# RMS norms from row sums on 128x9 numbers, applied behind the projections, in a hybrid decoder step

## The reference, cut to what matters

```
def rms_norm(x, g):
    y = x * rsqrt(mean(x * x, axis=-1) + 1e-6)
    return y * g

mixed = (g_a * (o_nsa @ w_branch_nsa) + g_b * (o_gm @ w_branch_gm)) @ w_out
x = x + rms_norm(mixed, ln_mix_post)
h2 = rms_norm(x, ln_ffn_pre)
f = (silu(h2 @ w_ffn_gate) * (h2 @ w_ffn_up)) @ w_ffn_down
x = x + rms_norm(f, ln_ffn_post)
e = ple @ w_ple
x = x + rms_norm(sigmoid(x @ w_ple_gate) * e, ln_ple_post)
```

## Time and profile before

| | us |
|---|---|
| median of 3 runs (2498.2 to 2499.25) | 2499.18 |
| the profiled execution | 2501.11 |
| its span, first to last instruction | 2499.3 |

### The profile page before, as it was taken

How to read it: one execution, slowest core, us unless ns; L and a number is a source line. 1 busy time by engine, 2 the same in 40 slices (tenths; PEclk the granted TensorE clock), 3 DMA queues, 4 the chain that set the end, 5 groups by cost and what they waited for, 6 DMA issues and landing times. The chain is left out here.

```text
span 2499.3 us, 33749 instructions
## 1 busy us (share of the span) xinstructions
PE 2152.2 (86%) x13578; PEld 2008.8 (80%) x13578; DVE 767.1 (31%) x1412; ACT 491.0 (20%) x881; POOL 628.7 (25%) x487
## 2 busy tenths in 40 slices
PE   7999799688768888799997909999999999992992
PEld 6999799587656667688887808999999999992882
DVE  3006233121256676311114184100111111127116
ACT  4111022100126656300102121111000100011121
POOL 2224100000024444212113123323323323223122
PEclk8999799756669999899998959999999999996996
DMA  5241431224020000111111221111111111120111
GB/s 179 61 148 39 127 136 59 79 102 168 6 110 2 1 1 1 34 50 38 38 42 51 84 85 51 40 45 51 50 38 55 42 37 56 44 100 28 40 34 68
DMA packets 164092, 151.17 MB, mean 60 GB/s; under 512 B 24010, under 2 KB 156555, under 8 KB 161156
## 3 DMA queue, kind: packets, MB, share of 16 engines
q1 hardware_dynamic: 160308, 116.41, 15.2%
q0 software_dynamic: 2304, 33.56, 3.5%
q10 hardware_dynamic: 1392, 0.01, 0.0%
HBM read 133.04 MB, written 21.10 MB: 62 GB/s over the span
## 5 line engine op out<-in xcount | busy, mean ns | idle before, releaser
L500 PE MATMUL ffn_acc<-HH,WS 128*128 128x344 f32 x2112 | 393.9, 321 | 21.2 <-POOL WS L510 18.8
L508 POOL CAST WS<-W 128x1024 fp32r<-128x1024 f32 (+2 forms) x126 | 129.8, 1030 | 1092.8 <-PE ffn_acc L500 508.8
L500 PEld LDWEIGHTS ffn_acc<-HH,WS 128*128 128x128 f32 x2112 | 344.7, 189 | 23.4 <-POOL WS L510 19.8
L510 POOL TENSOR_TENSOR WS<-W,WS 128x1024 fp32r<-128x1024 f32 (+2 forms) x126 | 293.5, 2330 | 10.1
L500 PE MATMUL ffn_acc<-HL,WS 128*128 128x344 f32 x1056 | 224.8, 321 | 0.0
L500 PE MATMUL ffn_acc<-AH,WS 128*128 128x344 f32 x1056 | 195.4, 320 | 0.0
L500 PE MATMUL proj_acc<-HH,WS 128*128 128x344 f32 x912 | 174.4, 324 | 7.6 <-DVE HL L474 7.6
L500 PEld LDWEIGHTS ffn_acc<-HL,WS 128*128 128x128 f32 x1056 | 179.4, 190 | 0.0
L1721 POOL TENSOR_SCALAR Hr<-Hr,tiny,gtok 128x63 f32<-128x63 f32 (+4 forms) x192 | 125.1, 661 | 185.4 <-DVE tiny L1801 141.5
L500 PEld LDWEIGHTS ffn_acc<-AH,WS 128*128 128x128 f32 x1056 | 171.7, 188 | 0.0
L2133 DVE TENSOR_TENSOR E<-E,ffn_acc 128x1032 f32<-128x1032 f32 x22 | 27.1, 1230 | 469.9 <-PE ffn_acc L500 469.9
(11 more groups left out here) (354 smaller groups left out, 3328.8 us busy)
## 6 DMA issues: line engine op xcount, KB each, us to landing
W<-in_w_in SPq DMA_DIRECT2D x31, 512.0 KB, 4.2
W<-in_w_ffn_gate SPq DMA_DIRECT2D x22, 512.0 KB, 3.8
W<-in_w_ffn_up SPq DMA_DIRECT2D x22, 512.0 KB, 3.8
X<-kept_x SPq DMA_DIRECT2D x2, 4128.0 KB, 13.2
W<-in_w_ffn_down SPq DMA_DIRECT2D x16, 384.0 KB, 3.4
W<-in_w_ffn_down SPq DMA_DIRECT2D x16, 320.0 KB, 3.2
kept_x<-Z SPq DMA_DIRECT2D x1, 4128.0 KB, 13.9
Z<-kept_x SPq DMA_DIRECT2D x1, 4128.0 KB, 13.0
```

What stands on the lines that cost most here:

```text
L500: last = k.nc.tensor.matmul(acc[:, s, n, 0:NW], k.WS[:, ws, part, c, :], src[:, c, n * NW:(n + 1) * NW], start=(c == 0 and part == 0 and s ...
L508: k.nc.gpsimd.tensor_copy(k.WS[:, ws, 0, 0:nk, :], w).then_inc(hi_done, 1)
L510: k.nc.gpsimd.tensor_tensor(k.WS[:, ws, 1, 0:nk, :], w, k.WS[:, ws, 0, 0:nk, :].bitcast(F32), ALU.subtract).then_inc(split_done, 1)
```

## The change

The four `norm_stage` calls go. `row_sums` takes the mean of the squares with tokens on the partitions: for each of nine token blocks the squares are the stationary operand and one column of 1/1024 moves, so that the result is 128x9. `RowRoot` adds eps, takes the reciprocal and the root on these numbers, and `row_spread` turns them back into a 128x1032 pattern in PSUM.

- Out-projection's norm: sums and spread at the head of `ffn`, then chunk by chunk scale, add and split (`first_tile` and the lists of ACT and DVE beside it).
- The FFN's pre-norm: only the gain stands ahead of the projections; the squares of each chunk are summed on PE between the chunks of the first gate tile, and the root (`k.R1`) is applied to the gate's result twice, ahead of the silu and behind it.
- The FFN's post-norm: at the head of `ple`, chunk by chunk.
- The last norm: the gain is applied to `k.F` in the loop of `ple`; x and F are both transposed in `store_y`, and there the root is a scale per token.
- The first tile of w_out is fetched and split at the end of `merge`; `out_projection` is written out instead of looped, ACT squares from PSUM and then copies. x is spilled by ACT's queue in `ffn`.

```diff
         merge(k)
         out_projection(k)
-        norm_stage(k, "mix_post", k.MX, residual=1, onto=k.MT, known=True)
-        norm_stage(k, "ffn_pre", k.X, spill=True)
         ffn(k)
-        norm_stage(k, "ffn_post", k.F, residual=3, onto=k.X, known=True)
         ple(k)
-        norm_stage(k, "ple_post", k.F, residual=4, onto=k.X, known=True)
         store_y(k)
...
+def row_sums(k, ps, sq, first=True, last=True):
+    for t in range(9):
+        m = P if t < TT else B
+        x = k.nc.tensor.matmul(ps[0:m, t:t + 1], sq[:, t * P:t * P + m], k.ones[:, 0:1], start=first, stop=last)
+    return x
+def row_spread(k, flat, rs):
+    for t in range(9):
+        m = P if t < TT else B
+        x = k.nc.tensor.matmul(flat[:, t * P:t * P + m], rs[0:m, t:t + 1].to_broadcast([m, P]), k.ident[0:m, 0:m], start=True, stop=True)
+    return x
+class RowRoot:
+    def __init__(self, k, st, name):
+        self.k = k
+        self.rs = k.tiny[:, 0:9]
+        self.cleared, self.mean, self.inverse, self.rooted = st.sems(" ".join(f"{name}_{x}" for x in ("cleared", "mean", "inverse", "rooted")))
+    def clear(self, dve):
+        self.k.nc.vector.memset(self.rs[:, TT:TT + 1], 1.0).then_inc(self.cleared, 1)
+    def vector(self, dve, ps):
+        nc = self.k.nc
+        dve.wait_ge(self.cleared, 1)
+        dve.wait_ge(self.mean, 1)
+        nc.vector.tensor_scalar(self.rs[:, 0:TT], ps[:, 0:TT], EPS, None, ALU.add).then_inc(self.inverse, 1)
+        nc.vector.tensor_scalar(self.rs[0:B, TT:TT + 1], ps[0:B, TT:TT + 1], EPS, None, ALU.add).then_inc(self.inverse, 1)
+        dve.wait_ge(self.inverse, 2)
+        nc.vector.reciprocal(self.rs, self.rs).then_inc(self.inverse, 1)
+    def scalar(self, act):
+        act.wait_ge(self.inverse, 3)
+        self.k.nc.scalar.activation(self.rs, self.rs, ACT.Sqrt).then_inc(self.rooted, 1)
...
+            sp.wait_ge(split_done, 17)
+            sp.dma_start(k.W[:, 0, 0:8, :], weight(g["w_out"], 0)).then_inc(k.wfull[0], 16)
...
+            pool.wait_ge(k.wfull[0], base[0] + 8 * 32 + 16)
+            pool.wait_ge(scaled, 2 + 15)
+            split_weights(k, pool, 0, 0, DC, hi_done, 16, split_done)
...
-            with sp.Fori(0, 4) as i:
-                for s in range(2):
-                    sp.wait_ge(split_done, 2 * i + s + 1)
-                    sp.dma_start(k.W[:, s, :, :], weight(g["w_out"], (2 * i + s) * P)).then_inc(k.wfull[s], 16)
+            for m in range(1, 8):
+                if m >= 3:
+                    sp.wait_ge(split_done, m - 2)
+                sp.dma_start(k.W[:, m % 2, :, :], weight(g["w_out"], m * P)).then_inc(k.wfull[m % 2], 16)
             sp.wait_ge(m_lo, DC)
             sp.dma_start(k.Z[:, 0:DC * N], k.kept).then_inc(x_back, 16)
             sp.wait_ge(x_back, 16)
...
+            for m in range(1, 8):
+                pool.wait_ge(k.wfull[m % 2], base[m % 2] + 16 * ((m + 1) // 2 if m % 2 else m // 2))
+                if m >= 2:
+                    pool.wait_ge(mm_done, m - 1)
+                split_weights(k, pool, m % 2, m % 2, DC, hi_done, m - 1, split_done)
...
+            for m in range(8):
+                if m:
+                    pe.wait_ge(split_done, m)
+                if m >= 2:
+                    pe.wait_ge(acc_free, m - 1)
+                split_tile(k, acc, m % 2, m % 2, k.HH, k.HL, DC, wait=(pe, m_lo) if m == 0 else None).then_inc(mm_done, 1)
...
+            for m in range(8):
+                act.wait_ge(mm_done, m + 1)
+                squares.square(act, acc[:, m % 2, :, 0:NW], m, m % 2)
+                nc.scalar.activation(tokens(k.MX[:, m, :]), acc[:, m % 2, :, 0:NW], ACT.Copy).then_inc(acc_free, 1)
+            act.wait_ge(acc_free, 8)
...
         done = (gate_done, up_done)
-        free = (silu_done, gated)
+        free = (scaled, gated)
         SL = k.E[:, 0:N]
         GU = k.E[:, N:2 * N]
-        h = NormSplit(k, st, 2, k.E[:, 0:N])
+        h = GainSplit(k, st, 2, k.MT)
+        roots = [RowRoot(k, st, "mix"), RowRoot(k, st, "pre")]
+        zeros = k.E[:, 5400:5409]
+        flat = acc[:, 1].rearrange("p n w -> p (n w)")[:, 0:N]
...
+        def first_tile(pe):
+            row_sums(k, aux[:, 0, 0:9], k.ssq).then_inc(roots[0].mean, 1)
+            pe.wait_ge(roots[0].rooted, 1)
+            row_spread(k, flat, roots[0].rs).then_inc(spread, 1)
+            pe.wait_ge(zeroed, 1)
+            nc.tensor.matmul(aux[:, 1, 0:9], k.ident[:], zeros, start=True, stop=False)
+            pe.wait_ge(split_done, 3)
+            for c in range(DC):
+                pe.wait_ge(h.lo_done, c + 1)
+                last = split_tile(k, acc, 0, 0, k.HH, k.HL, c + 1, first=c, more=c < DC - 1)
+                if c == DC - 1:
+                    last.then_inc(gate_done, 1)
+                pe.wait_ge(squared2, c + 1)
+                row_sums(k, aux[:, 1, 0:9], k.sq[:, c % 2, :], first=False, last=False).then_inc(summed2, 1)
+            nc.tensor.matmul(aux[:, 1, 0:9], k.ident[:], zeros, start=False, stop=True).then_inc(roots[1].mean, 1)
+            pe.wait_ge(roots[1].rooted, 1)
+            pe.wait_ge(mixed, DC)
+            row_spread(k, flat, roots[1].rs).then_inc(spread, 1)
+            pe.wait_ge(r_copied, 1)
...
-            h.scalar(act)
+            roots[0].scalar(act)
+            for c in range(DC):
+                act.wait_ge(x_new, c + 1)
+                h.scalar(act, c)
+                if c >= 2:
+                    act.wait_ge(summed2, c - 1)
+                nc.scalar.activation(k.sq[:, c % 2, :], k.MT[:, c, :], ACT.Square).then_inc(squared2, 1)
+            act.dma_start(k.kept, k.Z[:, 0:DC * N]).then_inc(spilled, 16)
+            roots[1].scalar(act)
+            act.wait_ge(spread, 2)
+            nc.scalar.activation(k.R1[:], flat, ACT.Copy).then_inc(r_copied, 1)
+            act.wait_ge(spilled, 16)
             for nf, m0, t0, s0, d0 in parts:
                 with act.Fori(0, nf) as m:
-                    act.wait_ge(gate_done, m + (m0 + 2))
-                    act.wait_ge(gated, m + (m0 + 1))
-                    nc.scalar.activation(tokens(SL), acc[:, 0, :, 0:NW], ACT.Silu).then_inc(silu_done, 1)
...
-            h.vector(dve)
+            nc.vector.memset(zeros, 0.0).then_inc(zeroed, 1)
+            roots[0].clear(dve)
+            roots[0].vector(dve, aux[:, 0, 0:9])
+            dve.wait_ge(spread, 1)
+            for c in range(DC + 1):
+                if c < DC:
+                    nc.vector.scalar_tensor_tensor(out=k.MX[:, c, :], in0=k.MX[:, c, :], scalar=k.gains[:, 1, c:c + 1], in1=flat,
+                                                   op0=ALU.mult, op1=ALU.mult).then_inc(mixed, 1)
+                    dve.wait_ge(mixed, c + 1)
+                    nc.vector.tensor_tensor(k.MT[:, c, :], k.MT[:, c, :], k.MX[:, c, :], ALU.add).then_inc(x_new, 1)
+                if c:
+                    dve.wait_ge(x_new, c)
+                    h.vector(dve, c - 1)
+            roots[1].clear(dve)
+            roots[1].vector(dve, aux[:, 1, 0:9])
+            dve.wait_ge(r_copied, 1)
+            dve.wait_ge(spilled, 16)
             for nf, m0, t0, s0, d0 in parts:
                 with dve.Fori(0, nf) as m:
+                    dve.wait_ge(gate_done, m + (m0 + 2))
+                    dve.wait_ge(gated, m + (m0 + 1))
+                    nc.vector.tensor_tensor(tokens(SL), acc[:, 0, :, 0:NW], tokens(k.R1[:]), ALU.mult).then_inc(scaled, 1)
                     dve.wait_ge(silu_done, m + (m0 + 2))
+                    nc.vector.tensor_tensor(SL, SL, k.R1[:], ALU.mult).then_inc(rescaled, 1)
+                    dve.wait_ge(rescaled, m + (m0 + 1))
                     dve.wait_ge(up_done, m + (m0 + 2))
...
+        ptok = k.E[:, 0:9 * 256].rearrange("p (t f) -> p t f", f=256)
...
+        root = RowRoot(k, st, "post")
+        flat = acc[:, 1].rearrange("p n w -> p (n w)")[:, 0:N]
...
+            row_sums(k, acc[:, 0, 0, 0:9], k.ssq).then_inc(root.mean, 1)
+            pe.wait_ge(root.rooted, 1)
+            row_spread(k, flat, root.rs).then_inc(spread, 1)
...
+                pe.wait_ge(mixed, DC)
...
+            root.scalar(act)
             for c in range(DC):
+                if c < 6:
+                    f, q = c // 3, c % 3
+                    act.wait_ge(tr_done, c + 1)
+                    a, w = (q * 512, 512) if q < 2 else (T, B)
+                    nc.scalar.activation(pT[:, f, a:a + w], tp[:, c % 2, 0:w], ACT.Copy).then_inc(tr_copied, 1)
+                act.wait_ge(x_new, c + 1)
                 nc.scalar.activation(k.HH[:, c, :], k.X[:, c, :], ACT.Copy).then_inc(x_hi, 1)
...
+                act.wait_ge(squares.squared, m + 1)
+                nc.scalar.activation(one(k.F, m), one(k.F, m), ACT.Copy, scale=k.gains[:, 4, bass.ds(m, 1)]).then_inc(scaled, 1)
...
+            root.clear(dve)
+            root.vector(dve, acc[:, 0, 0, 0:9])
+            dve.wait_ge(spread, 1)
+            for c in range(DC + 1):
+                if c < DC:
```

(61 more changed lines are left out.)

52 lines of the change are left out of this document (9 added, 43 removed).

## The result

The changed kernel takes 2411.0 us (median; 2408.7 to 2415.0) against 2499.2 for the kernel before beside it: a ratio of 0.9647, with a 95% interval from 0.963 to 0.9664. The direction was right and the size was not: 88 us came off instead of 67. The profiled execution took 2408.7 us, its span is 2406.9, against 2501.1 and 2499.3.

A forecast was written before the change was run, and what follows sets the result against it. PE, busy 86% of the span, was taken as the bound, with four holes where savings count one for one. Gains 9.0 + 14.2 + 23.1 + 20.8 = 67.1 us gave 2434.0 profiled, 2432.1 median; range 2418 to 2446.

The forecast's parts named there:

- Where PE waits: Three holes at the late norm stages and a 13.48 us one ahead of the out-projection; savings there shorten the span one for one.
- Ahead of the out-projection, 9.0: Merge and out-projection: early weight fetch and split start PE 7.8 us earlier, squaring from PSUM saves 1.2; together 9.0 us.
- Steps 1 to 4: Head of the FFN: row sums 3.7 us, root 1.2 with handoffs, spread 3.9, then DVE's three passes, 3.8 per chunk.
- Step 5: First FFN gate tile: PE at 1.2 GHz throughout, 6.25 us per chunk of 9 tile products and 18 row-sum records.
- The tail of the tile: Behind the first gate tile: last sums 3.65 us, closing product 0.4, root 1.2, spread 3.9, ACT's copy into R1 1.0.
- The loop at no cost: FFN loop: two more DVE passes, about 2.5 us per gate tile, hidden by the up tile's 11.4; cost 0.
- FFN to PLE, 23.1: FFN's end to first PLE gate tile: PE starts at T1 + 27.6, tile ends at T1 + 43.0 instead of 66.1; gain 23.1 us.
- The store, 20.8: Behind the PLE: 144 transposes, ninth block turned at T2 + 25.8, end at T2 + 32.8 instead of 53.6; gain 20.8 us.
- The spill: FFN: x's spill moves to ACT's queue, landing 13.9 us after about T0 + 54, before R1 is there.
- PE is granted 2.4 GHz in the first tile: First FFN tile: DVE then bounds, up tile ends near T0 + 62, 24 us more gained, 2408; one in ten.
- The late chunk chains: FFN and PLE heads: POOL's splits stretch several DVE steps, 5 to 8 us in each, 2442 to 2448; one in ten.
- The early split: End of merge: weight split moved into the last merge tile; the rival, not early, loses 7.8 us, 2440; three in a hundred.

The follow-up runs named there:

- fillers: Wide products nobody reads, put where PE waits; added to the changed kernel in all the gaps: 2406.4 us, ratio 0.9622.

## Why the prediction was wrong, step by step

- **Where PE waits.** Right. All of the gain came out of the four holes, one for one.
- **Ahead of the out-projection, 9.0.** Right, 8.9. The first output product started 4.1 us behind the last merge pass (1322.49 to 1326.61) instead of 12.0.
- **Steps 1 to 4.** Nearly right. Sums 3.68 (3.7 forecast), root 0.87 (1.2), spread 4.31 (3.9). DVE's first pass starts at T0' + 9.3 (8.9), a chunk is 3.67 (3.8). POOL's split stretched the first add to 2.83 us, 1.6 more where I had 0.6, so PE had its first chunk at T0' + 17.2, not 15.8.
- **Step 5, the failed step.** The sizes at either clock were right: at 1.2 GHz 6.21 against 6.25, at 2.4 GHz 3.43 against 3.3. The clock was not. From the earlier trace rows, narrow records alone and 4 transposes to 8 records, I went to "the same blend in longer pieces", and took that as no difference. It compared shares of time, and the wide part of those rows were transposes of 128 columns, here products of 344. The runs show that pieces and amount both matter: one piece of 18 records behind nine wide products runs at 2.4 GHz, three short pieces with the same work at 1.2, and 24 records at 1.2 after one fast chunk. One in ten for the fast case was too little for a question on which my rows said nothing direct, and the range should have reached 2408.
- **The tail of the tile.** From the end of the tile's products to the up tile 8 us instead of 10.5, since the last sums ran at the full clock.
- **The loop at no cost.** Right: 731.3 us from the up tile to the end of the FFN in both, with `L2223` and the pass behind it in it. The same 731.3 in the kernel with the old loop (1525.14 to 2256.4).
- **FFN to PLE, 23.1.** Right, 23.4; the tile ended at T1' + 42.7 (43.0 forecast), PE started at 28.2 (27.6).
- **The store, 20.8.** The mechanism was right: two blocks at the lower clock, turned at T2' + 7.4 and 9.7 (7.2 and 10.2), then 2.25 a block (2.3), the ninth at 25.3 (25.8). The term that was mis-sized is the tail: 7.0 forecast, 4.6 measured. I took the 5.9 us of the kernel before and added a pass. But those 5.9 us held a queue of output. Before, the blocks left every 1.1 us or so, and the DMA engines were still full when the last copy had ended; now they leave every 2.25 us, and the engines keep up. From DVE's last pass to the end it was 4.6 us (2494.70 to 2499.3) and is 2.15 (2404.75 to 2406.9), with a last block of 8 tokens in both. The DMA share, last column but one, before and then after:

```profile
2495.00:2498.00 3.00, 0.00 (x0) 0.00 (x0) 0.00 (x0) 0.00 (x0) 0.00 (x0) 1.00 1.02 403
2403.00:2406.00 3.00, 0.00 (x0) 0.00 (x0) 1.21 (x1) 0.44 (x1) 0.00 (x0) 0.99 0.51 186
```

- **The spill.** The 13.9 us were read from the wrong row: that transfer, of the same size, starts at 26.8 us, in the input projection; the spill that moved took 11.6 us before. No row shows when the new one lands. It is issued at 1462.16, the DVE pass that waits for it starts at 1475.38, 0.3 us behind the copy of R1, and PE waits only for R1, so it cost the path nothing.
- **The rivals.** "PE is granted 2.4 GHz in the first tile" came true, at 2408 by its own sum, and with its own end near T0 + 62 (64.1). The late chunk chains came true in one add of each stage, 1.6 and 1.5 us, and no further. The early split was early, and the loop hid its passes.
- **What the page says.** The Trainium skill (TensorE: Matmul & The Clock Gate, "Part 1: The HAM clock gate") says that activity lifts the throttle. Read as "a busy PE gets its clock" it gave the right time here for the wrong reason: the 29.5 us at 0.50 with PE busy for all of them speak against it, the half-idle PE at 1.00 as well.

What stays open: why one long and three short pieces of the same work differ, why 24 records a chunk lose what 18 keep, why a fast start made the changed tile fall once, and how other widths behave. The runs show that the clock differs, not what draws the line.

## What to carry to other kernels

Where a sum hangs on PE's clock and the rows at hand have another pattern of wide and narrow work, take both levels as cases of like weight and let the range hold both: here it was 22 us of 67. In this kernel narrow float32 records (one moving column, a full weight load) did best in one piece a chunk behind the wide products, and the fewer the better; other patterns weren't measured, so look at the granted clock of the stretch after each edit, for 0.65 us more of them a chunk cost 24.5 here. And read small parts from the rows, since the medians move by as much as they are worth.

## What the runs showed of the hardware

- PE fully busy is no ground for 2.4 GHz: 29.5 of 29.5 us busy at 0.50 with 9 wide products and 24 narrow records by turns. And PE busy for 7.49 of 15 us, with 9 wide products and 2 records by turns, has 1.00.
- A row-sum record takes 0.204 us at 1.2 GHz (18 in 3.68) and 0.109 at 2.4 (18 in 1.97).
- Nine wide products and 18 records by turns had 1.00 from the second chunk to the last in all eight profiles without fillers ahead of them (1444 to 1470 in the first). With fillers ahead, the same pattern fell to 0.50 for 6.00 of 6.00 busy us and came back.
- A fast start didn't help the short pieces: after 8 us at 1.00 and a wait of 1.72 us the clock fell in their first chunk and didn't come back before the tile's end.
- A DVE add of 1.23 us took 2.83 and 3.25 us beside POOL's subtraction of 2.34.
